# When the convolution taps are turned, and behind which prompt heads four condition blocks stand

## Time and profile before

| | |
|---|---|
| runs, median | 1215.69 us (1213.45 to 1216.23) |
| profiled execution, its own time | 1214.23 us |
| its span, first to last instruction | 1212.5 us |
| TensorE busy | 1177.5 us, 97% |
| VectorE, ScalarE, GpSimd busy | 687.4, 574.5, 421.1 us |
| DMA | 325.17 MB, mean 268 GB/s |
| granted TensorE clock | 0.99 of full |

### The profile page before, as it was taken

How to read it: one execution, slowest core, us unless ns; L and a number is a source line. 1 busy time by engine, 2 the same in 40 slices (tenths; PEclk the granted TensorE clock), 3 DMA queues, 4 the chain that set the end, 5 groups by cost and what they waited for, 6 DMA issues and landing times.

```text
span 1212.5 us, 28260 instructions
## 1 busy us (share of the span) xinstructions
PE 1177.5 (97%) x11603; PEld 1101.0 (91%) x11603; DVE 687.4 (57%) x1334; ACT 574.5 (47%) x736; POOL 421.1 (35%) x243
## 2 busy tenths in 40 slices
PE   8998999989999999999999999999999999999997
PEld 7998999979988787787789999999999999999997
DVE  3553444535544546633545548589999895683112
ACT  3643333223354444432333237676777775574443
POOL 1174656200000002200000002366677679606773
PEclk9999999999999999999999999999999999999998
DMA  9999999998899878899999998585857445455542
GB/s 320 317 349 296 348 345 365 358 384 304 285 324 312 275 251 290 260 369 337 334 372 354 302 284 290 201 286 164 280 169 251 141 156 184 136 171 162 165 140 95
DMA packets 242658, 325.17 MB, mean 268 GB/s; under 512 B 12436, under 2 KB 162788, under 8 KB 242116
## 3 DMA queue, kind: packets, MB, share of 16 engines
q1 hardware_dynamic: 218412, 284.60, 70.8%
q10 hardware_dynamic: 22470, 32.94, 8.2%
q0 software_dynamic: 1648, 5.82, 1.5%
HBM read 317.96 MB, written 7.06 MB: 268 GB/s over the span
## 4 chain that ended last, share of the span: by engine, by line
PE 79%; DMA 9%; DVE 5%; SPq 4%; issue 2%; ACT 1%; POOL 0%; DVEq 0%; ACTq 0%
PE PS L316 18%; PE PS L320 18%; PE PS L319 18%; DMA XR<-in_ada_w 9%; PE PS L418 5%; PE PS L1032 4%; SPq L396 3%; PE PS L1059 3%; PE PS L1290 2%; PE PS L718 2%; DVE PS L1818 2%; PE PS L719 2%; PE PS L720 2%; SPq L402 1%; PE PS L2022 1%
## 5 line engine op out<-in xcount | busy, mean ns | idle before, releaser
L316 PE MATMUL PS<-HH,WHI 128*128 128x288 f32 x1792 | 546.3, 305 | 7.6 <-issue 3.5
L320 PE MATMUL PS<-HH,WLO 128*128 128x288 f32 x1792 | 529.4, 295 | 0.0
L319 PE MATMUL PS<-HL,WHI 128*128 128x288 f32 x1792 | 529.2, 295 | 0.0
L310 POOL TENSOR_TENSOR WLO<-WRAW,WHI 128x1024 fp32r<-128x1024 f32 x155 | 373.2, 2423 | 335.0 <-ACT WHI L305 334.6
L305 ACT ACTIVATE WHI<-WRAW 128x1024 fp32r<-128x1024 f32 x272 | 284.6, 1055 | 346.8 <-PE PS L320 222.4
L316 PEld LDWEIGHTS PS<-HH,WHI 128*128 128x128 f32 x1792 | 337.8, 189 | 17.2 <-issue 13.7
L319 PEld LDWEIGHTS PS<-HL,WHI 128*128 128x128 f32 x1792 | 338.0, 189 | 0.0
L320 PEld LDWEIGHTS PS<-HH,WLO 128*128 128x128 f32 x1792 | 337.4, 188 | 0.2 <-issue 0.2
L310 DVE TENSOR_TENSOR WLO<-WRAW,WHI 128x1024 fp32r<-128x1024 f32 x117 | 144.6, 1238 | 134.1 <-ACT WHI L305 133.3
L1818 DVE SCALAR_TENSOR_TENSOR PS<-ACTS,CWT,PS 128x288 f32<-128x288 f32 x448 | 192.5, 514 | 4.2 <-ACT PS L1803 3.4
L718 PE MATMUL PS<-HH,WHI 128*128 128x288 f32 x384 | 115.3, 300 | 0.4 <-POOL WLO L310 0.4
(11 more groups left out here) (289 smaller groups left out, 929.6 us busy)
## 6 DMA issues: line engine op xcount, KB each, us to landing
XR<-in_ada_w SPq DMA_DIRECT2D x192, 512.0 KB, 8.9
WRAW<-in_c_w_in SPq DMA_DIRECT2D x96, 512.0 KB, 3.8
XR<-in_cache_b_k SPq DMA_DIRECT2D x128, 256.0 KB, 5.5
XR<-in_cache_b_v SPq DMA_DIRECT2D x128, 256.0 KB, 5.6
WRAW<-in_ab_w_in ACTq DMA_DIRECT2D x62, 512.0 KB, 7.0
WRAW<-in_ab_w_in SPq DMA_DIRECT2D x50, 512.0 KB, 7.7
WRAW<-in_ab_w_out SPq DMA_DIRECT2D x32, 512.0 KB, 9.7
WRAW<-in_c_w_out SPq DMA_DIRECT2D x32, 512.0 KB, 3.5
```

Of the source, the lines that this page charges most:

```text
L310: eng.tensor_tensor(WLO[:, c], WRAW[:, c], WHI[:, c].bitcast(F32), ALU.subtract).then_inc(w_lo[c], 1)
L316: first = pe.matmul(out, whi, HH[:, k, :], start=start, stop=False)
L319: pe.matmul(out, whi, HL[:, k, :], start=False, stop=False)
L320: return pe.matmul(out, wlo, HH[:, k, :], start=False, stop=stop)
```

## The change

1. The load of the taps moves from the end of ScalarE's small loads (issued at 5.45 us) to behind its `hi_load(act, 1)`, before the page table's load.
2. The four transposes of the taps leave `start_pe` and stand behind chunk 12 of the first stage; the ten unread products in front of the last quarter of block 0 become six.
3. VectorE's copy to `CWT` leaves the start and stands in step 13 of the first stage; its wait count before `ada_home(0)` falls from 3 to 2.
4. The sums of blocks 12 to 15 stand behind the first chunk of heads 1, 3, 5 and 7. VectorE brings them home at the end of steps 2, 4, 6 and 8.

```diff
@@ start_act
             hi_load(act, 1)
+            act.dma_start(CWROW, c_conv_w[0]...).then_inc(s_cw, 16)
             act.dma_start(PTAB, page_table...).then_inc(s_ptab, 16)
@@ small_loads
             act.dma_start(VROWS2, ada_b...).then_inc(s_vec, 16)
-            act.dma_start(CWROW, c_conv_w[0]...).then_inc(s_cw, 16)
@@ start_pe
             ada_quarter(pe, 0, 0, M0, 2)
-            pe.wait_ge(s_cw, 16)
-            for t in range(4):
-                last = pe.transpose(PS[:, M1, 124 * t:124 * t + 124], CWROW[:, t, :], IDENT[0:124, 0:124])
-            last.then_inc(s_cwt, 1)
             pe.wait_ge(xt_cp, KC)
-            keep_warm(pe, ACC[3], 10)
+            keep_warm(pe, ACC[3], 6)
             ada_quarter(pe, 0, 0, M0, 3)
@@ start_dve
-            dve.wait_ge(s_cwt, 1)
-            dve.tensor_copy(CWT[:], PS[:, M1, 0:KC * CW]...).then_inc(s_setup_cp, 1)
-            dve.wait_ge(s_setup_cp, 3)
+            dve.wait_ge(s_setup_cp, 2)
             ada_home(dve, 0, 0, M0)
@@ part_products
+            if i == 12:
+                pe.wait_ge(s_cw, 16)
+                for t in range(4):
+                    last = pe.transpose(PS[:, M1, 124 * t:124 * t + 124], CWROW[:, t, :], IDENT[0:124, 0:124])
+                last.then_inc(s_cwt, 1)
             if i in SUM_AT:
@@ qkv_dve
+                if i == 13:
+                    dve.wait_ge(s_cwt, 1)
+                    dve.tensor_copy(CWT[:], PS[:, M1, 0:KC * CW]...)
@@ prompt_pe
-                if h in (0, 2, 4, 6):
+                if h in (1, 3, 5, 7):
                     ada_sum(pe, 12 + h // 2, 12 + h // 2, M1)
@@ prompt_dve
-                    ada_home(dve, 12 + h // 2, 12 + h // 2, M1)   # in the branch of the odd heads
+                if h in (2, 4, 6, 8):
+                    ada_home(dve, 11 + h // 2, 11 + h // 2, M1)
```

More of the change, by code:

```diff
@@ L498, in start_act @@
             hi_load(act, 1)
+            act.dma_start(CWROW, c_conv_w[0].rearrange("w (k p) -> (w k) p", p=P).rearrange("(t r) p -> r t p", t=4)
+                         ).then_inc(s_cw, 16)
             act.dma_start(PTAB, page_table.rearrange("(a s) t -> a (s t)", a=1)).then_inc(s_ptab, 16)
@@ L518, in small_loads @@
             act.dma_start(VROWS2, ada_b.rearrange("l (k p) -> (l k) p", p=P)).then_inc(s_vec, 16)
-            act.dma_start(CWROW, c_conv_w[0].rearrange("w (k p) -> (w k) p", p=P).rearrange("(t r) p -> r t p", t=4)
-                         ).then_inc(s_cw, 16)
         XSQ = [A(HOFF, D), A(HOFF + D, D), A(HOFF, D, NS * DS)]
@@ L607, in start_dve @@
             link(dve, "dve", dve.tensor_copy(SLROW, PS[:, M2, 288:289]))
-            dve.wait_ge(s_cwt, 1)
-            dve.tensor_copy(CWT[:], PS[:, M1, 0:KC * CW].rearrange("p (w k) -> p k w", k=KC)).then_inc(s_setup_cp, 1)
-            dve.wait_ge(s_setup_cp, 3)
+            dve.wait_ge(s_setup_cp, 2)
             ada_home(dve, 0, 0, M0)
@@ L787, in qkv_dve @@
                     lows(dve, SUM_AT[i - 1])
+                if i == 13:
+                    dve.wait_ge(s_cwt, 1)
+                    dve.tensor_copy(CWT[:], PS[:, M1, 0:KC * CW].rearrange("p (w k) -> p k w", k=KC))
                 if i == 46:
```

## The result

| | kernel before | changed kernel |
|---|---|---|
| median, us | 1213.84 (6 runs) | 1204.70 (6 runs, 1203.88 to 1209.55) |
| ratio, 95% interval | | 0.9931 (0.9910 to 0.9953) |
| ratio in two later groups | | 0.9918 (0.9901 to 0.9936), 0.9927 (0.9904 to 0.9950) |
| profiled execution, us | 1214.23 | 1208.64 |
| its span, us | 1212.5 | 1206.9 |

The change is faster, by 8.4 to 10.0 us, where 6.0 were forecast; 1204.7 lies under the low end of the range, 1206.0. Against the forecast time, 1209.7, the distance is 5.0 us. Of it 1.9 is the anchor, which was luck of the draw: the three runs shown had a median of 1215.69, six have 1213.84, and later groups of 11 to 29 runs 1212.8 to 1214.9. From 1213.84 the low end of the range would be 1204.2. The other 3.1 is gain that the sum did not have.

A forecast was written before the change was run, and what follows sets the result against it. TensorE, busy 97%, was taken as the bound, the transfers as much so up to block 3. Part 1's 1.8 us (3.3 - 1.5) and part 2's 4.2 made 6.0: 1215.69 to 1209.7 us, range 1206 to 1215.

The forecast's parts named there:

- The start: Up to block 0's last quarter: without the taps' load, transposes and four products, the first product begins 3.3 us earlier.
- rival D: At the start: the taps hold some engines, so every block waits for these; part 1 is 4, time 1207.5; chance 0.13.
- The floor: At the first product: transposes (1.02 us) and four products (0.97) leave the chain, gaining at least 1.99 us.
- The queue: ScalarE's queue: chunk 5's load lands behind the moved taps, near 48.5 us, making modulation and chunk 6 late; charge 1.5 us.
- What passes block 3: At block 3's wait for its loads: 3.3 - 1.5 = 1.8 us of the gain is kept, being under the transfers' bound.
- The bound of 2.9 us from the idle engines: Up to block 3: transfers can come forward only by what they idled from 44 to 54 us, 2.9 us.
- Part 2: Block 12's sum behind head 1: waits -3.64, clock -1.7, cache stage's wait +1.1, together -4.2 us.
- The clock: Behind block 12's sum: 1.7 us more go with the idle stretch that pulled the clock to 0.50.
- The new wait: Start of the cache stage: it waits for block 15's home, now behind VectorE's take of head 7's output; +1.1 us.
- rival B: Blocks 12 to 15: later sums wait in block 12's place, 1 us each; time 1215.4, no change; chance 0.14.
- A: Up to block 3: the start's gain is given back entirely at the transfers; part 1 is 0, time 1211.5; chance 0.18.
- C: ScalarE's queue: the taps hold it, TensorE stands 11.2 us at chunk 5; part 1 +8, time 1219.5; chance 0.07.

The follow-up runs named there:

- e3: Kernel before with the taps' load made as two loads of 112 and 12 rows at its old place; median 1210.79 us, ratio 0.9983.
- e2: Kernel before with only the sums of blocks 12 to 15 moved behind heads 1, 3, 5, 7; median 1208.09 us, ratio 0.9974.
- e14: Kernel before with only the sums of blocks 12 to 15 moved behind heads 1, 3, 5, 7, second time; median 1207.74 us, ratio 0.9940.
- e4: Changed kernel with the taps' load alone put back to the end of ScalarE's small loads; median 1204.71 us, ratio 0.9936.
- e10: Changed kernel with ten unread products instead of six ahead of block 0's last quarter; median 1205.52 us, ratio 0.9932.
- part 1: Changed kernel with the sums of blocks 12 to 15 and their homes as before; medians 1210.88, 1210.18, 1209.53 us in three groups.
- e17: Kernel before with 8 unread products ahead of block 3's last quarter, 3 and 6 ahead of block 12's third and fourth; median 1213.48 us, ratio 1.0011.
- e12: Kernel before, unedited, run once more; median 1214.24 us, ratio 1.0005.
- e6: Changed kernel with the taps' load made as two loads of 112 and 12 rows at its new place; median 1203.09 us, ratio 0.9908.
- e8: Changed kernel with the taps loaded early in two pieces of 112 and 12 rows and block 15 brought home first; median 1200.73 us, ratio 0.9903.
- e16: Changed kernel with the taps loaded early in two pieces and block 15 brought home first, second time; median 1200.19 us, ratio 0.9885.

## Why the prediction was wrong

**The start, 3.3 us (upper end 4.4).** Measured 5.2 against the first trace, 3.6 against the five other executions with the old start. The step that failed is "0.112 x 10.1 / 1.08 = 1.05 us of everybody's time", a mean over 16 engines: block 0's last load landed 3.1 us earlier (24.5, before 27.6), not 1.05, and e3 shows it landing at 25.6 with the same bytes beside it, spread over more engines, which is worth 4.3 us at the first product (2.7 from the -1.5 of e2 and e14). It is rival D's mechanism. That 3.3 is near 3.6 is luck: the sum missed two thirds of the earlier landing, and it started from a trace whose third quarter was slow by 0.85 us. The rows had a sign of it that I passed over: the earlier trace rows shows 2.3 to 2.8 us for an issue, and I read only the landing. The floor, 1.99 us, was no floor: in e4 the last quarter waits for its load until 27.5 us, and only 0.9 us came beyond e2's start.

**The queue, -1.5 us.** The load did cost ScalarE's queue, by 5.85 us at the page table, which I had not thought of; chunk 5's load landed at 46.9 (48.5 forecast) and TensorE did not wait for it. The 49 packets per us were no measure of the taps either: from issue to the last landing they took 16.8 us (28.85 to 45.6) and not 10, as they had taken 15.8 in the kernel before. By chunk 12 all 5.2 us were gone. The charge was too small at its place, and wrong in kind: it is not added to what passes block 3, because block 3's load decides there.

**What passes block 3, 1.8 us.** In the pair of traces it was 3.5: the load lands 2.1 us earlier (96.5 to 94.4), the rest is the quarter at 1.08 instead of 1.93 and the products behind it at full clock. I had priced a low clock at block 12 and not here, with the 1.93 in the earlier trace rows. Averaged over executions the load lands 0.8 us earlier with the changed start (seven against six), and chunk 16 stands at -3.5 (seven) against -1.7 (four without fills): 1.8 us. With e10, whose start differs only by the four products, it would be 1.3. So the traces would bear out 1.8 or less, while the runs give part 1 3.8 us (2.3, 4.0, 5.0 in three groups): this term of the sum was too small by 2.0, the largest miss in it. Where the other 2 us arise stays open; e17 speaks against the clock as the whole answer. The bound of 2.9 us from the idle engines is not clearly broken. The split versions stand at -4.2 to -6.6 at chunk 16, but the unedited kernel stood at -4.0 in e12; counted in landings of block 3's last load from the mean of the six, 95.0, e3 and e6 gain 2.8 us and e8 and e16 3.6 to 3.7. If it is passed, it is by these two. The idle share is a mean over 16 engines too, which could be the reason and no run shows.

**The transposes at no cost** held: they took 0.59 us and moved chunk 13 by 0.35, inside block 3's wait. The four products at 0.97 us: 0.4 us at the first product, and nothing that could be seen in the time (e10).

**Part 2, -4.2 us.** Measured 5.2, mean of two groups of 3.2 and 7.3; 4.7 by the traces. Waits -3.64: on average 4.3 before, and 1.1 remain, since the margin of 0.2 us was crossed, as I said it could be. The clock, 1.7: right in kind at its place, where one pair of executions, e12 and e17, shows 3 us; the time of e17 did not bear it out. The new wait, 1.1: 0.97. Blocks 13 to 15 waited for their loads nowhere by more than 0.1 us, so rival B is out. The waits that go are 3.2 us on average, near 3.64. The term as a whole was too small by 1.0, against a mean of two groups whose intervals are wider than that.

**Rivals A and C.** A is half true: the gain from moving the load was given back (e4), the rest was not: part 1 alone won time in all three groups, where A had it at 0. C's mechanism was there, a held queue, with a wait of 2.2 us and not 11.

**Chances.** "Faster" had 0.77. The range ended 1.3 us too high because D and a part 2 above 4.2 were not allowed to meet: D's 4 and a part 2 of 5.2 give 1206.5 from the old anchor and 1204.6 from 1213.84.

## What to carry to other kernels

Ask of every load how many engines it uses, not how many bytes it has: 0.25 MB on four engines, as its semaphore records have it, held up 4 MB beside them, and two loads of 112 and 12 rows in its place were worth more than moving it (3.0 and 4.5 us under the changed kernel in two groups, by a version that also brings block 15 home first). Where a wait for a load stands at a fixed place, what is won or lost ahead of it is not by itself a term of the sum; the landing of that load is. Take the rows of one execution for mechanisms, and look at the spread of the runs before a size of 2 us is read from it.

## What was not expected of the hardware

- A small DMA behind a load on few engines took 5.85 us to issue (5.74 to 5.90 in seven more executions, 0.28 with the load split, 0.34 to 0.39 with it elsewhere), and its engine's instructions stood behind it.
- A long wait was mostly, not always, followed by a low clock. A quarter took 1.08 us after waits of 1.14, 1.86, 2.08 and 2.29 us, 1.62 after 2.42, 1.33 after 2.74, 1.61 after 3.10, 1.94 after 4.16, and yet 1.08 after 2.86 and 3.12, with the low clock just behind it. Once it was low it stayed so over a second, shorter wait (1.94 after 1.58 in e12).
- Two profiled executions of one kernel differed by up to 6 us at one place in the middle, and runs of it within one group by 10 us in the whole, with no edit.
